# FFN up products of a two-layer encoder: two wider passes in place of three per weight block

## The chip, the cores and the metric

One core of one Trainium2 chip runs the whole program. The metric is the device time of one execution in microseconds (us). Before the change it is 1035.1 us, the median of three runs (1034.61 to 1035.34).

## The reference

A bidirectional encoder trunk of two layers over 256 tokens of width 1024, in float32. Each layer is an attention sublayer (three mixers) and a gated MLP. The change is in the MLP and in the way its input is laid out:

```python
def conv_gated_mlp(h, w_up, conv_w, w_down):
    u = h @ w_up                                   # 256 x 1024 by 1024 x 5632
    up = jnp.pad(u, ((0, 0), (pad, pad), (0, 0)))
    u = sum(up[:, t:t + S] * conv_w[t] for t in range(CONV_WIDTH))   # 3 taps over the tokens
    gate, val = jnp.split(u, 2, axis=-1)
    return (jax.nn.gelu(gate, approximate=True) * val) @ w_down

h = rms_norm(x, ffn_pre_norm[l])
x = x + rms_norm(conv_gated_mlp(h, w_up[l], ffn_conv[l], w_down[l]), ffn_post_norm[l])
```

## The kernel before

Every float32 product is made of three passes on TensorE. Both operands are split into a high part and a low part (`hi` is the value rounded to the matmul's type, `lo` is the rest), and `passes` (L1404 to L1408) sums low by high, high by low and high by high in one PSUM bank.

Weights come in pieces of up to 128 x 2048 values through a ring of three buffers. SyncE issues the DMA of piece n when the low part of piece n-3 has been made. ScalarE makes the high part of a piece (`split_hi`, L702), VectorE the low part (`split_lo`, L1051). Both engines walk through the same hand-written list of steps: in the step of piece n they split piece n+2, so TensorE can begin piece n+2 only when VectorE has come through that part of step n (TensorE waits for `lo_done`).

The MLP of a layer has 22 up pieces, c = 0 to 21, each with 8 blocks of 128 input channels for 256 output channels, and 11 down pieces. Even c is the gate half and odd c the value half of a unit u = c // 2. The order of the pieces is c0 to c5, down 0, c6, c7, down 1, and so on to c20, c21, down 8, down 9, down 10: the first six up pieces run without a down piece between them, then two up pieces and one down piece make a period.

- TensorE, up piece (`use_piece`, L1482 on): 16 pairs (k, j) of input block and half of the output channels; each pair is three passes with a 128 x 128 weight block as the stationary operand and 256 token columns of `hT_hi` or `hT_lo` as the moving one, 48 matmuls in all. A whole piece fills one PSUM bank, and four banks take turns (`up_half`), so piece c waits only for the scaling of piece c-4.
- TensorE, down piece: 24 matmuls of 512 columns. It waits for its weights and for `g_lo` of its unit (`gated_lo`, L1116).
- VectorE, step of an up piece: `scale_up` (L1104) reads the bank and multiplies by the token scales (the norm's root, one per token) into `up_scaled`; for odd c `gated` (L1111) of the unit before; `split_lo` of piece n+2; for even c `gated_lo` of unit u-2; then, after ScalarE's middle tap, two outer taps of the convolution for each of two halves (L1356, L1362). In the step of a down piece it only does `split_lo`.
- ScalarE, step of an up piece: `split_hi` of piece n+2, then, once `up_scaled` is there, two middle taps (L948); for odd c the gelu (L954) and `gated_hi` (L833) of the unit before.
- The last units: in the step of down 8, VectorE does `gated_lo` of unit 9 first, then `gated` and, after a split, `gated_lo` of unit 10.
- The turn into the MLP ("mid"): TensorE transposes x (`turn_ffn`, L1615 on) of two token halves t into PSUM in four pairs of blocks each; ScalarE makes `hT_hi` (L814), VectorE `hT_lo` (`ffn_lo`, L1078) in the order `FFN_LO`. Up piece 0 waits for the low parts of both t before it uses a pair.
- For c = 0 the token scales are only there when TensorE, in the middle of piece 1, has turned the roots (`turn_roots`); VectorE copies them in `scale_rows` (L1093) before it scales piece 0.

Of the kernel before, what the change touches and what calls it, by code (L numbers as in the profile page):

```python
# [8 lines left out]
F32 = mybir.dt.float32  # L9
F32R = mybir.dt.float32r  # L10
# [6 lines left out]
P = 128  # L17
# [249 lines left out]

FFN_FULL = [(t, pair) for t in range(NT) for pair in range(4)]
FFN_HI = FFN_FULL
FFN_LO = [(t, pair) for pair in range(4) for t in range(NT)]  # L270

NPAR = 3 * FT * 2 + 22 + 1
PRE_A, PRE_F, G_Q, G_KV, G_SUB, LAM = 132, 140, 148, 151, 153, 154
# [18 lines left out]
def build_trunk(nc, a, out):  # L292
    with ExitStack() as ctx:
# [6 lines left out]

        sb("pad_512", [P, 96])
        x = sb("x_rows", [P, NT, D])
        hT_hi = sb("hT_hi", [P, KD, SEQ], F32R)
        hT_lo = sb("hT_lo", [P, KD, SEQ], F32R)
        raw = sb("w_raw", [P, RING, 2048])
        w_hi = sb("w_hi", [P, RING, 2048], F32R)
        w_lo = sb("w_lo", [P, RING, 2048], F32R)
# [66 lines left out]
            sb("pad_six", [P, 5120], scope=six)  # L374
            par_rows = sb("par_rows", [44, 4 * DEPTH, P], scope=six)

        bank = [ctx.enter_context(nc.psum_tensor(f"bank{i}", [P, 512], F32)) for i in range(8)]
        S_BANK, O_BANK = (bank[4], bank[5]), bank[7]

        def t_bank(n):  # L380
# [34 lines left out]
        squares, rstd_done = sem("squares"), sem("rstd_done")  # L415
        ffn_squares = sem("ffn_squares")
        root_rows_ready, scales_full, up_scaled_done = sem("root_rows_ready"), sem("scales_full"), sem("up_scaled_done")
        lat_squares, lat_normed = sem("lat_squares"), sem("lat_normed")
        attn_means, latent_means, latent_roots = sem("attn_means"), sem("latent_means"), sem("latent_roots")
        head_means, head_roots = sem("head_means"), sem("head_roots")  # L420
# [76 lines left out]

        def turned_bank(t, k):

            return bank[((0, 1, 6, 7), (2, 3, 5, 0))[t][k // 2]][:, (k % 2) * P:(k % 2 + 1) * P]  # L500

        def up_half(c, j):

            if c == 0:
                return bank[(4, 2)[j]][:, 0:SEQ]
            return bank[4 + c % 4][:, j * SEQ:(j + 1) * SEQ]

        root_rows = xn[:, 0, 0:NT * P].rearrange("p (t q) -> p t q", t=NT)
        token_scale = xn[:, 0, 512:512 + SEQ]
# [165 lines left out]
        def _(act):  # L675
# [182 lines left out]
            for l in range(DEPTH):  # L858
                for step in STEPS:
# [64 lines left out]
                    elif what == "pv":  # L924
                        g = step[1]
                        if g < 4 or g >= 8:
                            act.wait_ge(o_full, l * NPV + (g + 1))
                            if g < 4:
                                nc.scalar.activation(mla_oT[:, g, 0, :], O_BANK[:, 0:SEQ], ACT.Copy).then_inc(o_hi, 1)
                            else:  # L930
                                nc.scalar.activation(dil_oT[:, g - 8, 0, :], O_BANK[:, 0:SEQ], ACT.Copy).then_inc(o_hi, 1)
                    elif what == "w":
                        n = step[1]
                        kind, c, k0, nk, cols = PIECES[n]
                        if n + 2 < NPIECE and n != UP0 - 1 and (l == 0 or n):
                            split_hi(l, n + 2)
                        if kind == "out" and c == 0 and k0 == 4:
                            for t in range(NT):
                                post_square(l, 0, t, 0)
                        if kind == "up":  # L940
                            u, b = c // 2, c % 2
                            act.wait_ge(up_scaled_done, l * 2 * NU + (c + 1))
                            if b == 1 and u >= 2:

                                act.wait_ge(g_lo_done, l * NU + (u - 1))
                            for j in range(2):
                                ch = 22 * b + 2 * u + j
                                last = nc.scalar.activation(conv[:, u % 2, b, j * SEQ:(j + 1) * SEQ], up_scaled[:, c % 2, j, :], ACT.Copy,  # L948
                                                            scale=par_all[:, l, 44 + ch:45 + ch])
                            last.then_inc(conv_mid, 1)  # L950
                            if b == 1:

                                act.wait_ge(conv_done, BASE + l * 2 * NU + c)
                                nc.scalar.activation(conv[:, u % 2, 0, :], conv[:, u % 2, 0, :], ACT.Gelu_apprx_tanh).then_inc(gelu_done, 1)  # L954
                                if u:
                                    gated_hi(l, u - 1)
                        elif kind == "down" and c == NU - 1 - LAG:
                            gated_hi(l, NU - 1)
                        elif kind != "down" and k0 + nk == K_TOTAL[kind] and kind not in BY_DVE:
                            f = first_of(n)  # L960
                            for m in range(f, f + tiles_of(n)):
                                empty_tile(l, m)
# [4 lines left out]
        def _(dve):  # L967
# [127 lines left out]

            def scale_up(l, n, c):

                dve.wait_ge(piece_used, l * NPIECE + (RING + n + 1))
                if c == 0:
                    scale_rows(l)  # L1100
                    for j in range(2):
                        last = V.tensor_tensor(up_scaled[:, c % 2, j, :], up_half(c, j), token_scale, ALU.mult)
                else:
                    last = V.tensor_tensor(up_scaled[:, c % 2, :, :], bank[4 + c % 4][:].rearrange("p (j q) -> p j q", j=2),  # L1104
                                           token_scale.rearrange("p (o q) -> p o q", o=1).broadcast_to([P, 2, SEQ]), ALU.mult)
                last.then_inc(up_scaled_done, 1)

            def gated(l, u):

# [145 lines left out]
            for l in range(DEPTH):  # L1255

                for step in STEPS:
# [68 lines left out]
                    elif what == "w":  # L1326
# [13 lines left out]
                        elif kind == "up":  # L1340
# [6 lines left out]
                                split_lo(l, n + 2)  # L1347
                            if b == 0 and u >= 2:
                                gated_lo(l, u - 2)
                            dve.wait_ge(conv_mid, l * 2 * NU + (c + 1))  # L1350
                            dve.drain()
                            cv, src = conv[:, u % 2, b, :], up_scaled[:, c % 2, :, :].rearrange("p j q -> p (j q)")
# [10 lines left out]
                                                              in1=cv[:, o:o + SEQ - 1], op0=ALU.mult, op1=ALU.add)  # L1363
                            last.then_inc(conv_done, 1)
                        elif last_pair:
                            gated_lo(l, NU - 2)
                            dve.drain()
                            gated(l, NU - 1)
                            split_lo(l, n + 2)
                            dve.drain()  # L1370
                            gated_lo(l, NU - 1)
# [3 lines left out]
        def _(pe):  # L1375
# [94 lines left out]
            def use_piece(l, n):  # L1470
# [10 lines left out]
                pe.wait_ge(lo_done, l * NPIECE + (n + 1 + RING))  # L1481
                if kind == "up":  # L1482
                    u, b = c // 2, c % 2
                    if c >= 4:

                        pe.wait_ge(up_scaled_done, l * 2 * NU + (c - 3))
                    order = [(k, j) for k in range(8) for j in range(2)] if c == 0 else [(k, j) for j in range(2) for k in range(8)]
                    for k, j in order:
                        if c == 0 and j == 0 and k % 2 == 0:
# [1 line left out]
                            pe.wait_ge(turn_emptied, l * NTURN + (TURN_BEFORE["ffn"] + last_of + 1))  # L1491
                        if c == 1 and (k, j) == (0, 1):
                            turn_roots(l)
                        last = passes(up_half(c, j), (hi[:, k, j * P:(j + 1) * P], lo[:, k, j * P:(j + 1) * P]),
                                      hT_hi[:, k, :], hT_lo[:, k, :], k == 0, k == 7)
                    last.then_inc(piece_used, 1)
                    return
                halves = 2 if cols == 1024 else 1
# [116 lines left out]
            def turn_ffn(l, t):  # L1615

                pe.wait_ge(tile_emptied_dve, BASE + l * N_DVE + emptied_by_dve(post_tile(0, 1, t)))
                for k in range(KD):
                    if k % 4 == 0:
                        pe.wait_ge(x_ready, l * 8 + (X_START + 2 * t + k // 4 + 1))  # L1620
                    if t == 1 and k == 6:
                        pe.wait_ge(turn_emptied, l * NTURN + (TURN_BEFORE["ffn"] + FFN_LO.index((0, 0)) + 1))
                    last = PE.transpose(turned_bank(t, k), x[:, t, k * P:(k + 1) * P], ident[:])
                    if k % 2 == 1:
                        last.then_inc(turn_full, 1)
# [183 lines left out]
```

## Time and profile before

| what | value |
|---|---|
| median of three runs | 1035.1 us |
| the profiled execution | 1034.86 us |
| its span, first to last instruction | 1033.1 us |
| granted TensorE clock, mean | 0.998 |
| TensorE / VectorE / ScalarE busy | 98% / 66% / 57% |
| first and last matmul of the up products | 329.8 and 1008.1 us |

All times in the rows below are microseconds from the start of the span. A matmul's shown duration includes the time through the array, so the rate of the engine is read from the distance between two starts, not from the duration. The same holds for neighbouring instructions of VectorE and ScalarE, which overlap by some hundredths of a microsecond. The two layers repeat one another 507.75 us apart.

### The profile page before, as it was taken

What the parts mean: (1) busy time and instruction counts of PE and PEld (TensorE: products, weight loads), DVE (VectorE), ACT (ScalarE), POOL (GpSimd) and SP (SyncE); (2) the same over time, 40 slices, a digit from 0 to 9 for tenths busy, and PEclk for the clock granted to TensorE, in tenths of its full rate; (3) what the DMA queues carried; (4) which work ended last, traced back from release to release, by engine and by line L of the source; (5) the groups of instructions that cost most, each with busy time, mean ns of one, the idle gap of its engine ahead of it and who ended that gap; (6) DMA issues with size and microseconds to landing.
All of it is one profiled execution on the core that took longest, in us unless ns stands there. A gap on an engine that the chain in (4) does not pass through costs nothing.

```text
span 1033.1 us, 15933 instructions
## 1 busy us (share of the span) xinstructions
PE 1014.2 (98%) x6244; PEld 908.9 (88%) x6244; DVE 679.4 (66%) x932; ACT 587.3 (57%) x859; POOL 131.8 (13%) x257
## 2 busy tenths in 40 slices
PE   8999999999999999999999999999999999999996
PEld 7889999888878999999888899998888789999995
DVE  5635566655586887878775355656555869787876
ACT  5657666555436655555475666565553457555543
POOL 3353114000002000000024221230000020000000
PEclk9999999999999999999999999999999999999999
DMA  8555445454445656555554544464345545555551
GB/s 250 185 174 155 123 144 165 158 164 163 143 140 166 204 167 200 178 190 186 166 181 151 173 123 128 149 204 164 128 154 174 176 143 167 200 176 192 186 181 41
DMA packets 106222, 170.79 MB, mean 165 GB/s; under 512 B 3377, under 2 KB 72804, under 8 KB 106148
## 3 DMA queue, kind: packets, MB, share of 16 engines
q1 hardware_dynamic: 104860, 166.88, 49.6%
q10 hardware_dynamic: 1208, 2.63, 0.7%
q8 instruction: 50, 0.82, 0.3%
q0 software_dynamic: 80, 0.26, 0.1%
q14 instruction: 24, 0.20, 0.1%
HBM read 168.72 MB, written 1.05 MB: 164 GB/s over the span
## 4 chain that ended last, share of the span: by engine, by line
PE 90%; DVE 5%; DVEq 2%; ACT 1%; issue 1%; DMA 1%; SPq 0%; POOL 0%; POOLq 0%; ACTq 0%
PE bank L1406 26%; PE bank L1408 26%; PE bank L1407 26%; PE bank L1757 2%; DVE w_lo L1051 1%; PE bank L1658 1%; PE bank L1679 1%; DVEq L1250 1%; PE bank L1750 1%; DVE merged L1251 1%; PE bank L1667 1%; PE bank L1695 1%; PE bank L1702 1%; PE bank L1747 1%; DMA w_raw<-in_w_in_dram 1%
## 5 line engine op out<-in xcount | busy, mean ns | idle before, releaser
L1051 DVE TENSOR_TENSOR w_lo<-w_raw,w_hi 128x2048 fp32r<-128x2048 f32 (+3 forms) x174 | 364.1, 2095 | 173.2 <-ACT w_hi L702 173.0
L702 ACT ACTIVATE w_hi<-w_raw 128x2048 fp32r<-128x2048 f32 (+3 forms) x174 | 304.6, 1752 | 60.9 <-PE bank L1408 59.2
L1406 PE MATMUL bank<-w_hi,hT_lo 128*128 128x512 f32 (+2 forms) x700 | 258.4, 369 | 2.1 <-DVE hT_lo L1125 1.3
L1408 PE MATMUL bank<-w_hi,hT_hi 128*128 128x512 f32 (+2 forms) x700 | 252.9, 361 | 0.0
L1407 PE MATMUL bank<-w_lo,hT_hi 128*128 128x512 f32 (+2 forms) x700 | 252.5, 361 | 0.0
L1406 PE MATMUL bank<-hT_hi,w_lo 128*128 128x256 f32 x704 | 199.4, 283 | 0.7 <-DVE hT_lo L1078 0.7
L1408 PE MATMUL bank<-hT_hi,w_hi 128*128 128x256 f32 x704 | 199.2, 283 | 0.0
L1407 PE MATMUL bank<-hT_lo,w_hi 128*128 128x256 f32 x704 | 199.2, 283 | 0.0
L1406 PEld LDWEIGHTS bank<-w_hi,hT_lo 128*128 128x128 f32 x700 | 131.5, 188 | 18.3 <-issue 3.5
L1408 PEld LDWEIGHTS bank<-w_hi,hT_hi 128*128 128x128 f32 x700 | 131.4, 188 | 14.1
L1407 PEld LDWEIGHTS bank<-w_lo,hT_hi 128*128 128x128 f32 x700 | 131.6, 188 | 13.0
L1406 PEld LDWEIGHTS bank<-hT_hi,w_lo 128*128 128x128 f32 x704 | 135.1, 192 | 1.7 <-issue 1.1
L1407 PEld LDWEIGHTS bank<-hT_lo,w_hi 128*128 128x128 f32 x704 | 135.1, 192 | 0.6
L1408 PEld LDWEIGHTS bank<-hT_hi,w_hi 128*128 128x128 f32 x704 | 135.1, 192 | 0.0
L948 ACT ACTIVATE conv_out<-up_scaled,par_all 128x256 f32<-128x256 f32 x88 | 40.1, 502 | 147.3 <-DVE up_scaled L1104 136.5
L612 POOL TENSOR_SCALAR mean_squares<-small 128x1 f32<-128x1 f32 x12 | 7.8, 654 | 603.2 <-ACT x_normed L847 587.7
L1406 PE MATMUL bank<-w_hi,g_lo 128*128 128x512 f32 x176 | 68.9, 391 | 2.2 <-DVE g_lo L1116 2.2
L1407 PE MATMUL bank<-w_lo,g_hi 128*128 128x512 f32 x176 | 68.7, 390 | 0.0
L1408 PE MATMUL bank<-w_hi,g_hi 128*128 128x512 f32 x176 | 68.5, 389 | 0.0
L1104 DVE TENSOR_TENSOR up_scaled<-bank,x_normed 128x512 f32<-128x512 f32 x42 | 29.0, 691 | 59.1 <-PE bank L1408 59.1
L601 POOL TENSOR_TENSOR rope_a<-stage,cosT 128x96 f32<-128x96 f32 (+1 forms) x40 | 28.7, 717 | 164.9 <-ACT stage L721 136.2
L1356 DVE SCALAR_TENSOR_TENSOR conv_out<-up_scaled,par_all,conv_out 128x255 f32<-128x255 f32 x88 | 38.7, 481 | 6.0 <-ACT conv_out L948 2.1
(215 smaller groups left out, 1249.9 us busy)
## 6 DMA issues: line engine op xcount, KB each, us to landing
w_raw<-in_w_up_dram SPq DMA_DIRECT2D x44, 1024.0 KB, 4.9
w_raw<-in_w_in_dram SPq DMA_DIRECT2D x36, 1024.0 KB, 5.0
w_raw<-in_w_in_dram SPq DMA_DIRECT2D x36, 768.0 KB, 4.3
w_raw<-in_w_down_dram SPq DMA_DIRECT2D x22, 1024.0 KB, 4.8
w_raw<-in_w_out_dram SPq DMA_DIRECT2D x8, 1024.0 KB, 4.9
w_raw<-in_w_in_dram SPq DMA_DIRECT2D x8, 672.0 KB, 4.0
w_raw<-in_w_branch_mla_dram SPq DMA_DIRECT2D x4, 1024.0 KB, 4.8
w_raw<-in_w_branch_diff_dram SPq DMA_DIRECT2D x4, 1024.0 KB, 5.1
```

The source lines that it names most:

```text
L601: nc.gpsimd.tensor_tensor(ca, xr, c, ALU.mult)
L702: nc.scalar.activation(w_hi[:, n % RING, 0:nk * cols], raw[:, n % RING, 0:nk * cols], ACT.Copy).then_inc(hi_done, 1)
L948: last = nc.scalar.activation(conv[:, u % 2, b, j * SEQ:(j + 1) * SEQ], up_scaled[:, c % 2, j, :], ACT.Copy, scale=par_all[:, l, 44 + ch:4 ...
L1051: V.tensor_tensor(w_lo[:, n % RING, s], raw[:, n % RING, s], w_hi[:, n % RING, s].bitcast(F32), ALU.subtract).then_inc(lo_done, 1)
L1104: last = V.tensor_tensor(up_scaled[:, c % 2, :, :], bank[4 + c % 4][:].rearrange("p (j q) -> p j q", j=2), token_scale.rearrange("p (o q) ...
L1250: dve.drain()
L1251: last = V.tensor_tensor(merged[:, t, s], merged[:, t, s], gs, ALU.add)
L1356: V.scalar_tensor_tensor(out=cv[:, o + 1:o + SEQ], in0=src[:, o:o + SEQ - 1], scalar=par_all[:, l, ch:ch + 1], in1=cv[:, o + 1:o + SEQ], o ...
L1406: PE.matmul(dst, lhs[1], rhs_hi, start=start, stop=False)
L1407: PE.matmul(dst, lhs[0], rhs_lo, start=False, stop=False)
L1408: return PE.matmul(dst, lhs[0], rhs_hi, start=False, stop=stop)
L1757: last = PE.transpose(T_BANK[:, b * P:(b + 1) * P], probs[:, i % 2, b * P:(b + 1) * P], ident[:])
```

## The change

The high and the low part of the MLP's input now lie side by side in one buffer, `hT`, and one 512-column pass multiplies a block's high weights with both; the low weights go over the high input alone, in a 256-column pass into the first half of the same bank. Each up piece now fills two banks of 512 columns, and two such pairs of banks take turns, so piece c waits for the summing of piece c-2. ScalarE copies the second half of both banks to `up_scaled`, VectorE adds the first half to it, and a further VectorE instruction multiplies by the token scales. The order of the low parts of `hT` and the banks of the transposes change at the turn into the MLP, because banks 4 and 5 are now those of piece 0. `gated_lo` of unit 9 moves from the step of down 8 to the step of c21, ahead of its taps.

```diff
-FFN_LO = [(t, pair) for pair in range(4) for t in range(NT)]
+FFN_LO = [(0, 0), (0, 1), (1, 0), (1, 1), (0, 2), (1, 2), (0, 3), (1, 3)]
...
-        hT_hi = sb("hT_hi", [P, KD, SEQ], F32R)
-        hT_lo = sb("hT_lo", [P, KD, SEQ], F32R)
+        hT = sb("hT", [P, KD, 2, SEQ], F32R)
+        hT_hi, hT_lo = hT[:, :, 0, :], hT[:, :, 1, :]
...
-            return bank[((0, 1, 6, 7), (2, 3, 5, 0))[t][k // 2]][:, (k % 2) * P:(k % 2 + 1) * P]
+            return bank[((0, 1, 6, 7), (2, 3, 0, 1))[t][k // 2]][:, (k % 2) * P:(k % 2 + 1) * P]
+        def up_banks(c):
+            return up_bank[:, 2 * (c % 2):2 * (c % 2) + 2, :]
...
(ScalarE, step of an up piece, behind split_hi)
+                            act.wait_ge(piece_used, l * NPIECE + (RING + n + 1))
+                            if c >= 2:
+                                act.wait_ge(conv_done, BASE + l * 2 * NU + (c - 1))
+                            nc.scalar.activation(up_scaled[:, c % 2, :, :], up_banks(c)[:, :, SEQ:2 * SEQ], ACT.Copy).then_inc(up_copied, 1)
                             act.wait_ge(up_scaled_done, l * 2 * NU + (c + 1))
...
(VectorE, scale_up)
-                dve.wait_ge(piece_used, l * NPIECE + (RING + n + 1))
+                dve.wait_ge(up_copied, l * 2 * NU + (c + 1))
+                sums = up_scaled[:, c % 2, :, :]
+                V.tensor_tensor(sums, sums, up_banks(c)[:, :, 0:SEQ], ALU.add).then_inc(up_summed, 1)
                 if c == 0:
                     scale_rows(l)
-                    for j in range(2):
-                        last = V.tensor_tensor(up_scaled[:, c % 2, j, :], up_half(c, j), token_scale, ALU.mult)
-                else:
-                    last = V.tensor_tensor(up_scaled[:, c % 2, :, :], bank[4 + c % 4][:]..., token_scale..., ALU.mult)
-                last.then_inc(up_scaled_done, 1)
+                dve.drain()
+                V.tensor_tensor(sums, sums, token_scale..., ALU.mult).then_inc(up_scaled_done, 1)
...
(VectorE, step of an up piece, ahead of the taps; and the step of down 8)
+                            if c == 2 * NU - 1:
+                                gated_lo(l, NU - 2)
...
-                            gated_lo(l, NU - 2)
...
(TensorE, up piece)
-                    if c >= 4:
-                        pe.wait_ge(up_scaled_done, l * 2 * NU + (c - 3))
+                    if c >= 2:
+                        pe.wait_ge(up_summed, l * 2 * NU + (c - 1))
...
-                        last = passes(up_half(c, j), (hi[:, k, j * P:(j + 1) * P], lo[:, k, j * P:(j + 1) * P]),
-                                      hT_hi[:, k, :], hT_lo[:, k, :], k == 0, k == 7)
+                        into = up_banks(c)[:, j, :]
+                        PE.matmul(into, hi[:, k, j * P:(j + 1) * P], hT[:, k, :, :].rearrange("p s q -> p (s q)"),
+                                  start=k == 0, stop=False, skip_group_check=True)
+                        last = PE.matmul(into[:, 0:SEQ], lo[:, k, j * P:(j + 1) * P], hT_hi[:, k, :], start=False, stop=k == 7,
+                                         skip_group_check=True)
...
(TensorE, turn_ffn)
-                    if t == 1 and k == 6:
-                        pe.wait_ge(turn_emptied, l * NTURN + (TURN_BEFORE["ffn"] + FFN_LO.index((0, 0)) + 1))
+                    if t == 1 and k in (4, 6):
+                        pe.wait_ge(turn_emptied, l * NTURN + (TURN_BEFORE["ffn"] + FFN_LO.index((0, k // 2 - 2)) + 1))
```

## Rows read from the trace of the kernel before

**Rows 1.** The page, busy time of each engine, share of the span, instructions.

```profile
PE 1014.2 (98%) x6244; PEld 908.9 (88%) x6244; DVE 679.4 (66%) x932; ACT 587.3 (57%) x859; POOL 131.8 (13%) x257
```

**Rows 2.** Timeline of TensorE around one up and one down piece: start, duration, instruction.

```profile
376.12 0.28 PE L1406 MATMUL bank<-hT_hi,w_lo 128*128 128x256 f32 x1
...
381.88 0.40 PE L1406 MATMUL bank<-w_hi,g_lo 128*128 128x512 f32 x1
...
387.34 0.28 PE L1406 MATMUL bank<-hT_hi,w_lo 128*128 128x256 f32 x1
```

**Rows 3.** Timeline of VectorE over one period of three pieces; idle time and releaser in brackets.

```profile
376.32 0.69 DVE L1104 TENSOR_TENSOR up_scaled<-bank,x_normed 128x512 f32<-128x512 f32 x1 [3.60 <-PE bank L1408]
376.93 2.28 DVE L1051 TENSOR_TENSOR w_lo<-w_raw,w_hi 128x2048 fp32r<-128x2048 f32 x1
379.12 1.09 DVE L1116 TENSOR_TENSOR g_lo<-conv_out,g_hi 128x512 fp32r<-128x512 f32 x1
380.31 0.88 DVE L1356 SCALAR_TENSOR_TENSOR conv_out<-up_scaled,par_all,conv_out 128x255 f32<-128x255 f32 x2
381.26 0.88 DVE L1362 SCALAR_TENSOR_TENSOR conv_out<-up_scaled,par_all,conv_out 128x255 f32<-128x255 f32 x2
382.08 0.69 DVE L1104 TENSOR_TENSOR up_scaled<-bank,x_normed 128x512 f32<-128x512 f32 x1
382.69 0.68 DVE L1111 TENSOR_TENSOR conv_out<-conv_out 128x512 f32<-128x512 f32 x1
383.29 2.28 DVE L1051 TENSOR_TENSOR w_lo<-w_raw,w_hi 128x2048 fp32r<-128x2048 f32 x1
...
387.42 2.28 DVE L1051 TENSOR_TENSOR w_lo<-w_raw,w_hi 128x2048 fp32r<-128x2048 f32 x1
393.30 0.69 DVE L1104 TENSOR_TENSOR up_scaled<-bank,x_normed 128x512 f32<-128x512 f32 x1 [3.60 <-PE bank L1408]
```

**Rows 4.** Timeline at the end of the first layer, TensorE and VectorE.

```profile
506.27 1.06 DVE L1116 TENSOR_TENSOR g_lo<-conv_out,g_hi 128x512 fp32r<-128x512 f32 x1
...
507.47 0.47 PE L1406 MATMUL bank<-w_hi,g_lo 128*128 128x512 f32 x1 [1.11 <-DVE g_lo L1116]
...
507.78 0.39 PE L1407 MATMUL bank<-w_lo,g_hi 128*128 128x512 f32 x1
...
510.41 1.07 DVE L1116 TENSOR_TENSOR g_lo<-conv_out,g_hi 128x512 fp32r<-128x512 f32 x1
```

**Rows 5.** Timeline of eight transposes of 128 columns.

```profile
523.11 1.04 PE L1551 MATMUL bank<-ident,x_rows 128*128 128x128 f32 x8
```

**Rows 6.** ScalarE's groups by form: busy time, mean ns of one, idle time before.

```profile
L776 ACT ACTIVATE probsT<-bank 128x512 f32<-128x512 f32 x40 | 23.9, 597 | 31.5 <-PE bank L1757 31.5
```

**Rows 7.** Timeline at the turn into the MLP, first layer.

```profile
328.40 4.39 DVE L1078 SCALAR_TENSOR_TENSOR hT_lo<-bank,par_all,hT_hi 128x128 fp32r<-128x128 f32 x16
...
329.83 0.35 PE L1406 MATMUL bank<-hT_hi,w_lo 128*128 128x256 f32 x1 [0.34 <-DVE hT_lo L1078]
```

**Rows 8.** Timeline of VectorE in the first six up pieces, first layer.

```profile
336.56 2.28 DVE L1051 TENSOR_TENSOR w_lo<-w_raw,w_hi 128x2048 fp32r<-128x2048 f32 x1
339.25 0.49 DVE L1093 COPY x_normed<-bank 128x128 f32<-128x128 f32 x2 [0.42 <-PE bank L1467]
...
359.34 0.69 DVE L1104 TENSOR_TENSOR up_scaled<-bank,x_normed 128x512 f32<-128x512 f32 x1 [0.34 <-PE bank L1408]
```

**Rows 9.** Timeline of ScalarE in the same stretch and in the period.

```profile
341.42 1.90 ACT L702 ACTIVATE w_hi<-w_raw 128x2048 fp32r<-128x2048 f32 x1
...
345.01 1.28 ACT L954 ACT_TABLE_LOAD   x1
...
383.62 0.62 ACT L954 ACTIVATE conv_out<-conv_out 128x512 f32<-128x512 f32 x1
384.14 1.13 ACT L833 ACTIVATE g_hi<-conv_out 128x512 fp32r<-128x512 f32 x1
```

**Rows 10.** The page, DMA issues: count, size, median us from issue to landing.

```profile
w_raw<-in_w_up_dram SPq DMA_DIRECT2D x44, 1024.0 KB, 4.9
```

More of the change, by code:

```diff
@@ L375, in build_trunk @@
             par_rows = sb("par_rows", [44, 4 * DEPTH, P], scope=six)
-        bank = [ctx.enter_context(nc.psum_tensor(f"bank{i}", [P, 512], F32)) for i in range(8)]
+        bank = [ctx.enter_context(nc.psum_tensor(f"bank{i}", [P, 512], F32)) for i in range(4)]
+        up_bank = ctx.enter_context(nc.psum_tensor("up_bank", [P, 4, 512], F32))
+        bank += [up_bank[:, i, :] for i in range(4)]
         S_BANK, O_BANK = (bank[4], bank[5]), bank[7]
@@ L417, in build_trunk @@
         root_rows_ready, scales_full, up_scaled_done = sem("root_rows_ready"), sem("scales_full"), sem("up_scaled_done")
+        up_copied, up_summed = sem("up_copied"), sem("up_summed")
         lat_squares, lat_normed = sem("lat_squares"), sem("lat_normed")
@@ L498, in turned_bank @@
         def turned_bank(t, k):
-            return bank[((0, 1, 6, 7), (2, 3, 5, 0))[t][k // 2]][:, (k % 2) * P:(k % 2 + 1) * P]
[L502 to L506, printed above, removed]
+            return bank[((0, 1, 6, 7), (2, 3, 0, 1))[t][k // 2]][:, (k % 2) * P:(k % 2 + 1) * P]
+        def up_banks(c):
+            return up_bank[:, 2 * (c % 2):2 * (c % 2) + 2, :]
         root_rows = xn[:, 0, 0:NT * P].rearrange("p (t q) -> p t q", t=NT)
@@ L1096, in scale_up @@
             def scale_up(l, n, c):
-                dve.wait_ge(piece_used, l * NPIECE + (RING + n + 1))
+                dve.wait_ge(up_copied, l * 2 * NU + (c + 1))
+                sums = up_scaled[:, c % 2, :, :]
+                V.tensor_tensor(sums, sums, up_banks(c)[:, :, 0:SEQ], ALU.add).then_inc(up_summed, 1)
                 if c == 0:
                     scale_rows(l)
-                    for j in range(2):
-                        last = V.tensor_tensor(up_scaled[:, c % 2, j, :], up_half(c, j), token_scale, ALU.mult)
-                else:
-                    last = V.tensor_tensor(up_scaled[:, c % 2, :, :], bank[4 + c % 4][:].rearrange("p (j q) -> p j q", j=2),
-                                           token_scale.rearrange("p (o q) -> p o q", o=1).broadcast_to([P, 2, SEQ]), ALU.mult)
-                last.then_inc(up_scaled_done, 1)
+                dve.drain()
+                V.tensor_tensor(sums, sums, token_scale.rearrange("p (o q) -> p o q", o=1).broadcast_to([P, 2, SEQ]), ALU.mult).then_inc(up_scaled_done, 1)
             def gated(l, u):
```

## The prediction

> **What bounds the kernel now.** I began with the busy times of the page: TensorE is busy 98% of the span, VectorE 66%, ScalarE 57% [rows 1]. So TensorE sets the time, and an edit that shortens its work helps only as long as nobody else becomes late. The busy share can't say whether that holds in the MLP, so I went to the timelines of that stage.
>
> TensorE first. An up piece runs from 376.12 to 381.88, 5.76 us for 48 matmuls of 256 columns: 0.120 each. The down piece runs to 387.34, 5.46 us for 24 matmuls of 512 columns: 0.2275 each [rows 2]. The next up piece follows without a gap. A period of two up pieces and one down piece is 2 x 5.76 + 5.46 = 16.98 us, and VectorE's rows repeat at exactly that distance, 376.32 and 393.30 [rows 3].
>
> VectorE next, because TensorE can't begin a piece before VectorE has made its low part. Let E be the moment at which VectorE starts on an even up piece (376.32). It is 0.20 behind the start of TensorE's next matmul (376.12), so "TensorE's next piece starts at X" and "its consumer starts at X + 0.20" are the same event. From E on VectorE runs: scaling at +0, `split_lo` of the down piece +0.61, `g_lo` +2.80, taps +3.99 and +4.94, scaling of the odd piece +5.76, `gated` +6.37, `split_lo` of the next even piece +6.97 to +9.25, taps, `split_lo` +11.10 to +13.38, and then 3.60 idle [rows 3]. The first 5.76 of these have no idle time in them. The low part that TensorE needs at 387.34 (+11.02) is there at +9.25. What TensorE adds between a release and its steady rate is read at the end of the layer: `g_lo` is ready at 507.33, the first matmul starts at 507.47, the second at 507.78, so 0.14 and then 0.31 in place of 0.23, together 0.22 [rows 4]. The real slack of VectorE's chain is thus 11.02 - 9.25 - 0.22 = 1.55 us in a period of 16.98. The 3.60 idle are not spare in the same sense: they lie behind the instruction that TensorE waits for.
>
> **The change part by part.**
>
> *Passes.* A pair (k, j) was 3 x 0.120 = 0.360. Now it is one pass of 512 and one of 256 columns, 0.2275 + 0.120 = 0.3475 [rows 2]. The columns are the same, 768; what goes is what a matmul costs beside its columns, 0.0125. Sixteen pairs make a piece 5.56 instead of 5.76; all 44 pieces give at most 704 x 0.0125 = 8.8 us. Bounds for a pair, since no row alternates the two widths: 0.335 (0.2275 and bare columns, 0.2275 - 0.120 = 0.1075) and 0.360 (no gain). I take the sum of the two measured distances.
>
> How much a weight load costs decides this price. Eight transposes of 128 columns take 1.04, of which 0.28 is the last one's duration: (1.04 - 0.28) / 7 = 0.109 between starts [rows 5]. If such a load stood ahead of each stream, a matmul of 256 columns would take 0.109 + 0.1075 = 0.216; the rows show 0.120, so the load lies under the matmul before it, and taking one away gives back little. The Trainium skill (TensorE: Matmul & The Clock Gate, Part 3, The mechanism) says that a weight load overlaps matmuls in flight only when its row group differs; here all loads use the whole array, so by that rule each removed load would be worth its full price. The trace disagrees with it.
>
> *ScalarE's copy.* A link that was not in the chain. ScalarE waits for the piece, then copies 512 values from PSUM; the same form takes 0.597 [rows 6], and the hand-over adds about 0.03: +0.63 before VectorE can start. For odd pieces VectorE comes late anyway and the copy is hidden.
>
> *The add and the drain.* VectorE had one instruction of 512 for the scaling, 0.69, and 0.61 to the next start. Now it has an add (0.69, then the drain; drains in the period cost 0.07 to 0.10, as 380.31 + 0.88 to 381.26, so 0.78 to the next start) and a multiplication with all operands in SBUF, like `gated` (0.68, 0.60 to the next start) [rows 3]. That is 1.38 where 0.61 stood: +0.77 for each up piece. Bounds: 0.60 (a bare distance again, no drain) and 0.90.
>
> *The period.* All of this falls on VectorE's chain from E: copy 0.63, add, multiplication to +2.01, `split_lo` (2.19 to the next start), `g_lo` +4.20 to +5.29, taps +5.39 and +6.34, the odd piece's add +7.16, multiplication +7.94, `gated` +8.54, `split_lo` +9.14 to +11.42. TensorE would have wanted it at 5.56 + 5.46 - 0.20 = +10.82; it goes on at 11.42 + 0.22 = +11.64. The slack of 1.55 has been turned into a stall of 0.82, of which 0.15 comes already ahead of the down piece (its `g_lo` is ready at +5.29, TensorE effectively goes on at +5.51 instead of +5.36). The loop closes: the next even piece ends 5.56 later, and the next E is at 11.64 + 5.56 + 0.20 = +17.40. So a period takes 17.40 where it took 16.98: the copy, the add and the drain ask for 2.17, the shorter even piece gives 0.20 back and the slack 1.55; **+0.42**. The odd piece's 0.20 is lost in the stall. The rest of VectorE's step ends at +15.57 and is not late. ScalarE isn't late either: its `split_hi` for the even piece ends near +4.9, its copy of the odd piece can run at +5.56, and behind that come taps, gelu and `g_hi` as before [rows 9].
>
> *The first six up pieces.* There the relief of a down piece is missing and VectorE was nearly full before: it idled 0.34 ahead of piece 4 [rows 8]. Here each step must be followed. Piece 0 starts at 330.20, not 329.83: four low parts follow one another 0.271 apart ((4.39 - 0.32) / 15), and the pair that piece 0 needs is now finished by the sixth instruction, 328.40 + 5 x 0.271 + 0.31 = 330.07, plus 0.13 [rows 7]. Piece 2 ends at 330.28 + 3 x 5.56 + 0.43 for the roots = 347.39. VectorE comes out of `split_lo` at 338.84, adds piece 0, takes the roots at about 339.5 (339.25 before) [rows 8], and ends its taps at 343.6. ScalarE is held by the taps of piece 0, does `split_hi` until 343.5 [rows 9], and only then copies piece 1. From there: add at 344.15, `split_lo` of piece 3 to 347.81, piece 3 goes on at 348.03 (stall 0.64) and ends at 353.59. ScalarE loads the gelu's table (1.28) [rows 9], splits to 350.3 and copies piece 2 to 350.9; `split_lo` of piece 4 ends at 354.59 (stall 1.22). Piece 5 is released at 360.71 (stall 0.56), down 0 by its `g_lo` at 367.50 (stall 1.23; ScalarE's copy of piece 4 had to wait for its `split_hi`, to 362.8), piece 6 at 373.63 (stall 0.67). E of piece 6 comes at 379.61; it was 376.32 [rows 3]. Check: stalls 4.32, later start 0.37, seven shorter pieces -1.40: **+3.29**.
>
> *The periods* from E of piece 6 to E of piece 20: 7 x 0.42 = **+2.94**.
>
> *The end of a layer.* Before, TensorE waited 1.11 for `g_lo` of unit 9 ahead of down 9, and the last down piece ended 23.29 behind E of piece 20. Now `g_lo` of unit 9 follows `split_lo` ahead of the taps: ready at +12.42, down 9 effectively from +12.64 (before +12.37), end +18.10. But the taps, `gated`, a split and `g_lo` of unit 10 come behind it, one after the other as before [rows 4]: taps from +12.52 to +14.29, `gated` +14.36, split +14.97, `g_lo` ready at +18.42, down 10 effectively from +18.64, end +24.10: **+0.81**. Behind the taps, `g_lo` of unit 9 would be ready at +14.3 and the end 1.4 later; the move is worth that, but doesn't bring back what VectorE's lateness costs.
>
> *At no cost.* Two banks in turn instead of four: TensorE needs the sum of piece c-2, and that is there 2 us and more ahead in each step above. The order of transposes: pairs 2 and 3 of the second half wait for low parts at 328.95 and 329.5, their high parts come 0.1 later, and piece 0 asks for them only at 333; uncovered it would be that 0.1. Weight transfers: 4.9 us to landing [rows 10], issued when the low part of piece n-3 is made, over a period ahead of their use; if this failed, ScalarE's split would wait and each late microsecond would go to TensorE. The wider layout of `hT` is read and written by the same instructions; I find no row that prices the stride and take 0, with 0.1 us either way.
>
> *Sum.* 3.29 + 2.94 + 0.81 = 7.04 a layer, 14.1 for two. The profiled execution took 1034.86; it stands 0.24 below the median. 1034.86 + 14.1 = **1049.0 us**.
>
> **The rivals.** *A: TensorE sets the pace and the gain arrives.* For it: 98% busy, and VectorE idles 3.60 in each period. Against it: that idle time is behind the instruction on which TensorE waits. It decides at the chain: if copy, add and multiplication asked for 0.82 less than 2.17 + 0.20 in a period, no stall would be left; for mere equality with before, 0.42 less. Then 8.8 us are gained and 2 x 0.37 lost at the start of piece 0: 1034.86 - 8.1 = 1026.8.
>
> *B: the mixed pair costs three passes.* The two passes take 0.360 or more, because a load under 256 columns followed by a wide pass hides less. Each up piece is 5.76 again; the chain through the even piece lengthens by 0.20 in each period and by about as much in each early step, some 1.6 a layer: 1052.2.
>
> *C: loads at their full price*, the mechanism that the rows speak against: a pair costs 0.360 - 0.109 = 0.251, a piece 4.02. VectorE's chain stays, only the even piece in the loop shrinks by 1.54 more, about 8 times in a layer: 1049.0 - 2 x 8 x 1.54 = 1024.4. This is where the rule of the Trainium skill (the page on TensorE, as above) would lead.
>
> *D: the VectorE steps cost about as much less as to end near the old time*, with the chain still in the lead: 0.77 down to 0.50. Two by 0.27 off a period of 17.40 is 16.86, 0.12 under the old one, and some 2 of the 4.1 lost early and at the end remain: about 1037.
>
> **How the numbers follow.** Forecast 0.73, A 0.09, B 0.12, C 0.02, D 0.04. The range: from the forecast down, the extra VectorE time at 0.65 instead of 0.77 takes 0.24 off each of 7 periods and 0.12 off about 6 early and last steps, 4.8 us for both layers, and the pair at 0.335 takes 0.2 off each piece in the chain, 3.3 more: 1040.9. Upward, B and the extra time at 0.85: 1052.2 + 3.2 = 1055.4. I give 1040.0 to 1056.0. It leaves out A, C and part of D, and the far sides, together about 0.2. About 0.2% is what a measurement of this kernel tells from no change; faster by more: A, C, a part of D, 0.12; within: 0.02; slower: 0.86.
>
> **What would show it.** The distance between starts of a pair: 0.3475. VectorE without a long wait for the copy in odd steps, and E to E at 17.40. TensorE waiting for `w_lo` (L1051's successor) 0.6 to 0.7 ahead of each even piece and for `g_lo` near 0.1 ahead of down pieces, where before it waited for neither. E of piece 6 near 379.6. Wrong would be the forecast if E to E came at 16.58 (rival A), if the pair measured 0.36 (B) or 0.25 (C), or if TensorE waited for `up_summed`, which I hold to be free.

## The result: 1048.9 us, slower by 1.3%, and the profile after

The changed kernel takes 1048.9 us (median of four runs, 1048.76 to 1049.06), the kernel before 1035.2 in the same session. The ratio is 1.0134, 95% interval 1.0120 to 1.0147. The forecast was 1049.0.

From the page of the changed kernel, busy times and then the chain that ended last:

```profile
PE 1017.2 (97%) x5540; PEld 869.4 (83%) x5540; DVE 708.7 (68%) x974; ACT 610.8 (58%) x903; POOL 130.8 (12%) x257
...
PE 67%; DVE 20%; DVEq 6%; ACT 4%; issue 2%; DMA 1%; SPq 0%; POOL 0%; POOLq 0%; ACTq 0%
```

and the chain of the kernel before, for comparison:

```profile
PE 90%; DVE 5%; DVEq 2%; ACT 1%; issue 1%; DMA 1%; SPq 0%; POOL 0%; POOLq 0%; ACTq 0%
```

TensorE has 704 instructions less and is still busy 97% of the span [rows 1]; the busy share says nearly nothing. The chain says it: TensorE's part fell from 90% to 67%, VectorE's rose from 5% to 20%.

What TensorE waited for (us in total, times, longest), changed kernel:

```profile
PE up_bank L1500 <- DVE w_lo L1057: 7.4, 20, 0.8
PE bank L1411 <- DVE g_lo L1120: 3.6, 4, 1.4
...
PE up_bank L1500 <- DVE hT L1084: 0.3, 2, 0.2
```

Twenty waits for low weights that were not there before, ten in each layer, and none for `up_summed`: two banks in turn were enough. This view undercounts a wait, since a matmul's shown duration runs 0.16 into it, and the first matmul behind it is slow (0.34 to the next start, 390.89 to 391.23 below, where others take 0.23).

One period of the changed kernel, ScalarE's copy, VectorE and TensorE:

```profile
379.41 0.60 ACT L947 ACTIVATE up_scaled<-up_bank 128x512 f32<-128x512 f32 x1 [2.72 <-PE up_bank L1502]
...
380.04 0.69 DVE L1106 TENSOR_TENSOR up_scaled<-up_scaled,up_bank 128x512 f32<-128x512 f32 x1 [2.52 <-ACT up_scaled L947]
380.82 0.69 DVE L1110 TENSOR_TENSOR up_scaled<-up_scaled,x_normed 128x512 f32<-128x512 f32 x1
381.43 2.29 DVE L1057 TENSOR_TENSOR w_lo<-w_raw,w_hi 128x2048 fp32r<-128x2048 f32 x1
383.64 1.09 DVE L1120 TENSOR_TENSOR g_lo<-conv_out,g_hi 128x512 fp32r<-128x512 f32 x1
384.82 0.88 DVE L1362 SCALAR_TENSOR_TENSOR conv_out<-up_scaled,par_all,conv_out 128x255 f32<-128x255 f32 x2
385.77 0.88 DVE L1368 SCALAR_TENSOR_TENSOR conv_out<-up_scaled,par_all,conv_out 128x255 f32<-128x255 f32 x2
386.57 0.68 DVE L1106 TENSOR_TENSOR up_scaled<-up_scaled,up_bank 128x512 f32<-128x512 f32 x1
387.34 0.69 DVE L1110 TENSOR_TENSOR up_scaled<-up_scaled,x_normed 128x512 f32<-128x512 f32 x1
387.95 0.68 DVE L1115 TENSOR_TENSOR conv_out<-conv_out 128x512 f32<-128x512 f32 x1
388.55 2.28 DVE L1057 TENSOR_TENSOR w_lo<-w_raw,w_hi 128x2048 fp32r<-128x2048 f32 x1
...
390.89 0.50 PE L1500 MATMUL up_bank<-hT,w_hi 128*128 128x512 f32 x1 [0.31 <-DVE w_lo L1057]
391.23 0.28 PE L1502 MATMUL up_bank<-hT,w_lo 128*128 128x256 f32 x1
391.34 0.40 PE L1500 MATMUL up_bank<-hT,w_hi 128*128 128x512 f32 x1
...
396.64 0.40 PE L1500 MATMUL up_bank<-hT,w_hi 128*128 128x512 f32 x1
...
396.84 0.60 ACT L947 ACTIVATE up_scaled<-up_bank 128x512 f32<-128x512 f32 x1 [2.71 <-PE up_bank L1502]
```

Read it against [rows 3]. E, the moment at which an even up piece's consumer starts, is now the start of ScalarE's copy. From E, 379.41, the low weights of the next even piece are done at 390.83, +11.42, where they were done at +9.25. TensorE begins the piece 0.06 later, and E comes again at 396.84: a period of 17.43 in place of 16.98. VectorE still idles 2.52 in it, behind the instruction that TensorE waits for and ahead of the copy.

### The profile page after: what moved, and what is told of

It is laid out like the page before. It is cut to its first block, busy times and chain, and to the rows that moved or that the text cites. A ratio compares the mean times of both kernels' runs of the same rounds, so it can differ in the third digit from the quotient of the medians.

```text
span 1047.3 us, 14699 instructions
## 1 busy us (share of the span) xinstructions
PE 1017.2 (97%) x5540; PEld 869.4 (83%) x5540; DVE 708.7 (68%) x974; ACT 610.8 (58%) x903; POOL 130.8 (12%) x257
## 4 chain that ended last, share of the span: by engine, by line
PE 67%; DVE 20%; DVEq 6%; ACT 4%; issue 2%; DMA 1%; SPq 0%; POOL 0%; POOLq 0%; ACTq 0%
PE bank L1411 15%; PE bank L1413 15%; PE bank L1412 15%; DVE w_lo L1057 9%; PE up_bank L1500 7%; PE up_bank L1502 3%; DVE up_scaled L1110 3%; DVE up_scaled L1106 3%; PE up_bank L1765 2%; DVEq L1357 2%; ACT w_hi L703 1%; PE up_bank L1666 1%; PE up_bank L1687 1%; DVEq L1254 1%; ACT up_scaled L947 1%
## 5 line engine op out<-in xcount | busy, mean ns | idle before, releaser
L1411 PE MATMUL bank<-w_hi,hT 128*128 128x512 f32 (+2 forms) x700 | 258.4, 369 | 2.1 <-DVE hT L1129 1.3
L1500 PE MATMUL up_bank<-hT,w_hi 128*128 128x512 f32 x704 | 252.2, 402 | 7.8 <-DVE w_lo L1057 7.4
L1413 PE MATMUL bank<-w_hi,hT 128*128 128x512 f32 (+2 forms) x700 | 252.9, 361 | 0.0
L1412 PE MATMUL bank<-w_lo,hT 128*128 128x512 f32 (+2 forms) x700 | 252.5, 361 | 0.0
L1502 PE MATMUL up_bank<-hT,w_lo 128*128 128x256 f32 x704 | 197.6, 281 | 0.0
L1500 PEld LDWEIGHTS up_bank<-hT,w_hi 128*128 128x128 f32 x704 | 132.2, 188 | 48.3 <-DVE w_lo L1057 16.0
L1411 PEld LDWEIGHTS bank<-w_hi,hT 128*128 128x128 f32 x700 | 131.5, 188 | 18.2 <-issue 3.5
L1413 PEld LDWEIGHTS bank<-w_hi,hT 128*128 128x128 f32 x700 | 131.4, 188 | 14.0
L1412 PEld LDWEIGHTS bank<-w_lo,hT 128*128 128x128 f32 x700 | 131.7, 188 | 13.0
L1502 PEld LDWEIGHTS up_bank<-hT,w_lo 128*128 128x128 f32 x704 | 133.0, 189 | 0.0
L1106 DVE TENSOR_TENSOR up_scaled<-up_scaled,up_bank 128x512 f32<-128x512 f32 x44 | 30.1, 684 | 43.4 <-ACT up_scaled L947 43.2
L1411 PEld LDWEIGHTS bank<-w_hi,g_lo 128*128 128x128 f32 x176 | 33.0, 188 | 15.6 <-issue 7.4
```

The source lines that it names most:

```text
L1106: V.tensor_tensor(sums, sums, up_banks(c)[:, :, 0:SEQ], ALU.add).then_inc(up_summed, 1)
L1411: PE.matmul(dst, lhs[1], rhs_hi, start=start, stop=False)
L1412: PE.matmul(dst, lhs[0], rhs_lo, start=False, stop=False)
L1413: return PE.matmul(dst, lhs[0], rhs_hi, start=False, stop=stop)
L1500: PE.matmul(into, hi[:, k, j * P:(j + 1) * P], hT[:, k, :, :].rearrange("p s q -> p (s q)"), start=k == 0, stop=False, skip_group_check=True)
L1502: last = PE.matmul(into[:, 0:SEQ], lo[:, k, j * P:(j + 1) * P], hT_hi[:, k, :], start=False, stop=k == 7, skip_group_check=True)
```

## The experiments

Two theories stood against each other. *Chain*: the copy, the add and the drain make VectorE deliver low weights too late, and the order of its work counts. *Others*: the passes themselves, the two banks in turn, ScalarE's copy wherever it stands, or the mere amount of VectorE's work.

**Without the scaling** (it leaves out the multiply by the token scales for pieces 1 to 21):

```diff
-                V.tensor_tensor(sums, sums, up_banks(c)[:, :, 0:SEQ], ALU.add).then_inc(up_summed, 1)
+                added = V.tensor_tensor(sums, sums, up_banks(c)[:, :, 0:SEQ], ALU.add)
+                added.then_inc(up_summed, 1)
+                if c >= 1:
+                    dve.drain().then_inc(up_scaled_done, 1)
+                    return
```

> The changed kernel without VectorE's drain-and-multiply by the token scales for pieces 1 to 21 (the sum is passed on unscaled; only piece 0 is scaled, so the output is not the reference's). It takes about 0.6 us out of each VectorE step. Theory (VectorE's chain from the copy over add, multiply, taps to the low weights sets the period): the period falls from 17.44 us to TensorE's own 2 x 5.65 + 5.46 = 16.8 or close to it, the waits for low weights ahead of even pieces vanish, and the time falls by some 18 us, to about 1030. Rival (the loss comes from ScalarE's copy and the two pairs of banks taking turns, or from the passes): the multiply is covered, and the time stays at 1047 to 1049.

Measured: 1031.5 us, ratio to the kernel before 0.9968 (0.9956 to 0.9980). ScalarE's copies of even pieces, one period apart:

```profile
393.17 0.60 ACT L947 ACTIVATE up_scaled<-up_bank 128x512 f32<-128x512 f32 x1 [3.34 <-PE up_bank L1506]
...
409.97 0.60 ACT L947 ACTIVATE up_scaled<-up_bank 128x512 f32<-128x512 f32 x1 [3.38 <-PE up_bank L1506]
```

16.80, TensorE's own pace (two up pieces of 5.65 and a down piece of 5.46 are 16.76). The copy, the add, the banks and the passes are all still there. So none of them is the loss by itself: leaving out one short VectorE instruction per piece takes the whole loss in the periods away.

**Three passes again**, everything else as changed:

```diff
-                        PE.matmul(into, hi[:, k, j * P:(j + 1) * P], hT[:, k, :, :].rearrange("p s q -> p (s q)"),
+                        PE.matmul(into[:, 0:SEQ], hi[:, k, j * P:(j + 1) * P], hT_hi[:, k, :],
                                   start=k == 0, stop=False, skip_group_check=True)
+                        PE.matmul(into[:, SEQ:2 * SEQ], hi[:, k, j * P:(j + 1) * P], hT_lo[:, k, :],
+                                  start=False, stop=False, skip_group_check=True)
```

> The changed kernel, but the 512-column pass is issued as two passes of 256 columns into the two halves of the bank, so each pair has three passes again; everything else as changed. It prices the wide pass alone. In the changed kernel a mixed pair takes 0.353 between starts, three passes take 0.360. Theory: a piece grows by 0.1 us, of which one in each period and nearly all early ones count: +2 us, about 1051. Rival (mixed widths cost TensorE time, so that the wide pass is part of the loss): the time falls below 1048. Rival (a weight load is worth its full price, 0.109): the time rises by 10 us or more.

Measured: 1051.0 us, 2.1 above the changed kernel. The wide pass is a small gain, and no part of the loss. Loads at their full price, which would have cost 10 us or more here, are excluded.

**The low part of unit 9 behind the taps again:**

```diff
-                            if c == 2 * NU - 1:
-                                gated_lo(l, NU - 2)
...
                         elif last_pair:
+                            gated_lo(l, NU - 2)
                             dve.drain()
```

> The changed kernel with the low part of unit 9 back where it was, in the step of down 8, behind the taps of piece 21. Theory: down 9 is released later by taps and outer work, about 1.4 us a layer: +2.7 us, 1051.6. Rival (the move buys nothing, because down 10 waits for its own low part in any case): 1049.

Measured: 1054.1 us, 5.2 more than the changed kernel where 2.7 were expected, and an unusually wide spread: the four runs took 1050.9, 1053.4, 1054.8 and 1055.4 us, at mean granted clocks of 0.999, 0.997, 0.994 and 0.993. TensorE at the start of down 9 in the first layer:

```profile
516.40 0.76 PE L1410 MATMUL bank<-w_hi,g_lo 128*128 128x512 f32 x1 [3.30 <-DVE g_lo L1120]
516.97 0.63 PE L1411 MATMUL bank<-w_lo,g_hi 128*128 128x512 f32 x1
517.39 0.63 PE L1412 MATMUL bank<-w_hi,g_hi 128*128 128x512 f32 x1
517.82 0.63 PE L1410 MATMUL bank<-w_hi,g_lo 128*128 128x512 f32 x1
```

and the stretches before and behind it (start and end, length, busy time of each engine, then the granted clock, DMA share and GB/s):

```profile
508.00:512.00 4.00, 4.00 (x19) 3.31 (x18) 3.83 (x7) 1.59 (x5) 0.00 (x0) 1.00 0.42 151
516.00:520.00 4.00, 3.60 (x9) 2.91 (x10) 3.82 (x4) 2.38 (x2) 0.00 (x0) 0.57 0.18 66
520.00:524.00 4.00, 4.00 (x20) 3.27 (x19) 1.89 (x2) 0.21 (x1) 0.00 (x0) 1.00 0.74 223
```

Here 3.30 us of waiting were followed by a granted clock of 0.57, so mostly the lower level, 1.2 GHz, and 512 columns took 0.43 from start to start instead of 0.2275. In the second layer of the same run the wait was as long, and the clock stayed at 1.00:

```profile
PE bank L1410 <- DVE g_lo L1120: 3.3, 1, 3.3
...
1034.00:1037.00 3.00, 3.00 (x15) 2.47 (x14) 2.91 (x3) 1.14 (x1) 0.00 (x0) 1.00 0.00 0
```

The two layers tell the two parts of the price apart. From E of piece 20 to ScalarE's first read of the last down piece it is 21.55 us in the second layer, 1.25 more than in the changed kernel (20.30), and 23.15 in the first, 2.86 more (20.29). So the move that the change makes is worth 1.25 us a layer by the order of work, 2.5 in all, close to the 2.7 expected and to the 2.0 of the fastest run. The rest, 2.7 of the 5.2 us, came with the lower clock. The changed kernel, whose wait there is 1.4 us, showed 0.998 or 0.999 in all four of its runs.

**The copy twice**, on even pieces from 6 on, and on odd pieces from 7 on:

```diff
+                            if c >= 6 and c % 2 == 0:          # in the other kernel == 1
+                                nc.scalar.activation(xn[:, 1, (c // 2 % 2) * 512:(c // 2 % 2) * 512 + 512]..., up_banks(c)[:, :, SEQ:2 * SEQ], ACT.Copy)
                             nc.scalar.activation(up_scaled[:, c % 2, :, :], up_banks(c)[:, :, SEQ:2 * SEQ], ACT.Copy).then_inc(up_copied, 1)
```

> The changed kernel with ScalarE's copy of even pieces from 6 on made twice (the first time to a scratch buffer), some 0.50 us more ahead of the add. Theory (the copy of an even piece lies in the chain): each of 8 even pieces a layer adds 0.50, +8 us, 1057. Rival (the copy is hidden behind VectorE's or TensorE's other work): within 1 us of 1049.

> The same doubling of the copy for odd pieces from 7 on. Theory (VectorE comes to the odd piece late, so that copy is covered): within 0.5 us of 1048.9. Rival (every copy is in the chain): +8 us.

Measured: 1056.5 us for even pieces, 7.6 above the changed kernel, and 1049.0 for odd ones, no difference. The same instruction costs nearly its full distance of 0.50 in one place and nothing in the other. In the even run the next period's copy comes 17.91 later, where it was 17.43:

```profile
379.20 0.60 ACT L948 ACTIVATE x_normed<-up_bank 128x512 f32<-128x512 f32 x1 [2.71 <-PE up_bank L1504]
379.70 0.59 ACT L949 ACTIVATE up_scaled<-up_bank 128x512 f32<-128x512 f32 x1
...
397.11 0.60 ACT L948 ACTIVATE x_normed<-up_bank 128x512 f32<-128x512 f32 x1 [2.70 <-PE up_bank L1504]
```

**Low weights first.** VectorE's work is only reordered; the same edit was made to the kernel before as a control:

```diff
+                            early = c >= 4 and b == 0
+                            if splits and early:
+                                split_lo(l, n + 2)
                             scale_up(l, n, c)
...
-                            if splits and c:
+                            if splits and c and not early:
                                 split_lo(l, n + 2)
```

> The changed kernel with one reordering on VectorE: for even pieces from 4 on, the low weights of the piece after next are made ahead of the add and not behind the multiply, in the time in which VectorE waits for the piece. No work is added or left out. Theory (the period is lost to the order of work in VectorE's chain, not to its amount): 2.2 us leave the chain between the end of the even piece and the low weights of the next one, the period falls to TensorE's own 16.8, and the time falls by about 11 us, to 1038. Rival (VectorE's amount of work or its memory traffic is too large now): 1045 or more.

> The kernel before with the same reordering of VectorE, as a control. Theory (there the chain had 1.55 us of slack): no change, 1035.2 within 0.5. Rival (the reordering is a gain by itself): 1033 or less.

Measured: the changed kernel so reordered 1038.2 us, 10.7 less; the kernel before so reordered 1034.8 beside 1034.9, no change. VectorE from one even piece to the next:

```profile
391.44 4.49 DVE L1057 TENSOR_TENSOR w_lo<-w_raw,w_hi 128x2048 fp32r<-128x2048 f32 x2
396.47 0.69 DVE L1106 TENSOR_TENSOR up_scaled<-up_scaled,up_bank 128x512 f32<-128x512 f32 x1 [0.54 <-ACT up_scaled L947]
397.25 0.69 DVE L1110 TENSOR_TENSOR up_scaled<-up_scaled,x_normed 128x512 f32<-128x512 f32 x1
397.86 1.07 DVE L1120 TENSOR_TENSOR g_lo<-conv_out,g_hi 128x512 fp32r<-128x512 f32 x1
```

Both low weights now lie back to back (x2) in the time that was idle, 2.52 before, 0.54 now, and E follows E at 16.79. That the same amount of work runs at TensorE's pace when it stands elsewhere shows that order, not amount, was the loss in the periods. What is left against the kernel before is 3.4 us. By the traces the first six pieces are 3.0 longer in each layer than before, the seven periods together 1.3 shorter, and the end of the layer 0.07 longer.

**And the copies of pieces 1 and 2 ahead of the high weights:**

```diff
+                        late = kind == "up" and c in (1, 2)
-                        if n + 2 < NPIECE and n != UP0 - 1 and (l == 0 or n):
+                        if n + 2 < NPIECE and n != UP0 - 1 and (l == 0 or n) and not late:
                             split_hi(l, n + 2)
...
+                            if late:
+                                split_hi(l, n + 2)
```

> As the reordered changed kernel (low weights ahead of the add for even pieces from 4 on), and for pieces 1 and 2 ScalarE copies the piece ahead of making high weights. Theory (in the first six pieces the copy waits behind 1.9 us of high weights): another 3.5 us, about 1034.6, level with the kernel before. Rival (the early pieces are bound by VectorE's amount of work): no gain over the reordering alone.

Measured: 1035.1 us beside 1034.9, ratio 1.0002 (0.9993 to 1.0012): level with the kernel before. The waits for low weights ahead of pieces 4 and 5 are gone. In the MLP of the first layer these remain:

```profile
364.98 0.47 PE L1417 MATMUL bank<-w_hi,g_lo 128*128 128x512 f32 x1 [0.58 <-issue]
...
371.47 0.50 PE L1506 MATMUL up_bank<-hT,w_hi 128*128 128x512 f32 x1 [0.78 <-DVE w_lo L1060]
...
506.64 0.47 PE L1417 MATMUL bank<-w_hi,g_lo 128*128 128x512 f32 x1 [0.59 <-DVE g_lo L1123]
...
512.72 0.47 PE L1417 MATMUL bank<-w_hi,g_lo 128*128 128x512 f32 x1 [0.38 <-DVE g_lo L1123]
```

The first six pieces now take 1.3 to 1.5 more than before in a layer, and the periods give 1.3 back: that is why the kernel is level and not faster.

**Two more moves, together and one alone,** and the first of these kernels with three passes:

```diff
-                            early = c >= 4 and b == 0
+                            early = c == 5 or (c >= 4 and b == 0)      # not in the one with the gating move alone
...
-                            if b == 1 and u >= 1:
-                                gated(l, u - 1)
...
                             last.then_inc(conv_done, 1)
+                            if b == 0 and u >= 1:
+                                gated(l, u - 1)
```

> The reordered changed kernel with the copy of pieces 1 and 2 first, and two more moves on VectorE: the low weights of the piece after next are made first for piece 5 too, and the gating product of the unit before moves from the odd step to the end of the even step, where VectorE idles 1.2 us. No work is added or left out. Theory (what is left are single waits: 0.78 ahead of piece 6, about 0.5 and 0.6 ahead of down 9 and down 10, in each layer): 1.3 to 1.5 us a layer, so 1035.1 - 2.8 = 1032.3, faster than the kernel before by 0.25%. Rival (VectorE's work of the first six pieces is the bound, and the order only shifts the waits): 1034.5 or more.

> The same, with the 512-column pass again as two passes of 256 columns. Here TensorE sets the pace in most pieces, so the wide pass shows what it is worth. Theory: 0.360 - 0.3535 = 0.0065 for each of 704 pairs, 4.6 us, less what falls into the waits that are left: 4 us above the two-pass version. By the forecast's price of 0.0125 a pair it would be 8.8 us. Rival (mixed widths give nothing): equal.

> The kernel with low weights and early copies first (1035.1), plus the gating product moved to the end of the even step, without the move for piece 5. Theory (the run with both moves lost 1.8 us because low weights ahead of piece 5's add delay its taps and with them ScalarE's high weights for piece 7): the 1.7 us wait ahead of piece 7 is gone, and the time is 1034.3 to 1035.2. Rival (the early gating product itself costs): 1036.5 or more.

Measured: both moves 1036.9 us, ratio 1.0016 (1.0007 to 1.0025); the gating move alone 1034.65 beside 1034.88, ratio 0.9999 (0.9990 to 1.0008). The expectation of 1032.3 for both moves was wrong by 4.6, and its rival, that the order only shifts the waits (1034.5 or more), is what came. The wait ahead of piece 6 went, and a longer one came ahead of piece 7. Rows of the run with both moves, of the three engines:

```profile
371.80 0.91 ACT L957 ACTIVATE conv_out<-up_scaled,par_all 128x256 f32<-128x256 f32 x2 [4.26 <-DVE up_scaled L1113]
...
376.10 4.49 DVE L1060 TENSOR_TENSOR w_lo<-w_raw,w_hi 128x2048 fp32r<-128x2048 f32 x2 [1.45 <-ACT w_hi L703]
...
378.45 0.50 PE L1506 MATMUL up_bank<-hT,w_hi 128*128 128x512 f32 x1 [1.70 <-DVE w_lo L1060]
```

With low weights first, piece 5 is scaled 2.2 later than with the gating move alone; ScalarE, which works in order, stands 4.26 waiting for that (2.05 with the gating move alone) ahead of the high weights of piece 7; VectorE then waits 1.45 for these. The chain runs through both engines, so what is won ahead of one link on VectorE is paid for behind ScalarE. Without the move for piece 5 the loss was gone, as expected. With three passes the kernel with both moves takes 1040.3, 3.4 more, close to the 4 that were expected and far from the 8.8 of the forecast's price.

## Why the prediction was right, step by step

*What bounds it.* Right. The idle 3.60 of VectorE was not spare; the slack was 1.55, and the runs with low weights first and with the copy twice show the chain directly: the same work in another order takes the loss of the periods away, and 0.50 more in the even step costs 7.6 us in 16 pieces, in the odd step nothing.

*The period.* Forecast 17.40, measured 17.43. On VectorE every distance came as priced: copy and hand-over 0.63, add 0.78, multiply 0.61, low weights ready at +11.42 as forecast. Two terms beyond it were off and cancelled. A pair of passes takes 0.353, not 0.3475: from 391.34 to 396.64 are 15 pairs, 5.30 / 15. That is the mis-sized term of the sum: the wide pass gains about half of what the forecast gave it (0.0067 for each pair instead of 0.0125), and a piece is 5.65, not 5.56. The sum of the two distances of [rows 2] was too low. And TensorE started 0.06 behind its low weights, not 0.14. The forecast had read the 0.14 from a wait for `g_lo` [rows 4] and used it for `w_lo`; behind `g_lo` it is 0.14 in the changed kernel too, after a wait of only 0.36 (below). The 0.15 forecast ahead of the down piece did not show as a wait: `g_lo` was ready at 384.73, and TensorE came to it at 384.87.

```profile
518.81 1.06 DVE L1120 TENSOR_TENSOR g_lo<-conv_out,g_hi 128x512 fp32r<-128x512 f32 x1
...
520.01 0.47 PE L1411 MATMUL bank<-w_hi,g_lo 128*128 128x512 f32 x1 [0.36 <-DVE g_lo L1120]
```

*The first six pieces.* Forecast +3.29. E of piece 6 comes at 379.41; the run stands 0.15 ahead of the one before at the turn into the MLP (327.81 against 327.96 for the second half's transposes), so +3.24. Inside it the distribution was off: the wait of 0.64 ahead of piece 3 didn't come, since the pieces ahead of it were longer and VectorE could add piece 1 0.36 earlier than forecast. The waits came to 3.7 instead of 4.3, and the seven shorter pieces gave 0.8 instead of 1.4. These two go together: where VectorE's chain sets the end, a longer piece only eats into the wait behind it. The second layer, though, has only +2.90. The difference is a pause of 0.43 in VectorE's row of work in the taps of piece 4, for which the profile gives no reason; in the second layer the same instruction comes 0.34 earlier after the one before it, and so does everything behind it:

```profile
368.34 0.88 DVE L1368 SCALAR_TENSOR_TENSOR conv_out<-up_scaled,par_all,conv_out 128x255 f32<-128x255 f32 x2 [0.43 <-issue]
```

*The end of a layer.* Forecast +0.81. The first tile of the last down piece was read by ScalarE at 521.68, 20.29 behind E of piece 20 (501.39), before at 19.38 (495.18 to 514.56): +0.91.

```profile
521.68 0.60 ACT L848 ACTIVATE x_normed<-bank 128x512 f32<-128x512 f32 x1 [0.60 <-PE bank L1413]
```

Before:

```profile
514.56 0.60 ACT L847 ACTIVATE x_normed<-bank 128x512 f32<-128x512 f32 x1
```

*The sum, and the luck in it.* The same three stretches in both layers, us more than before:

| stretch | forecast | first layer | second layer |
|---|---|---|---|
| up to E of piece 6 | 3.29 | 3.24 | 2.90 |
| seven periods | 2.94 | 3.12 | 3.10 |
| end of the layer | 0.81 | 0.91 | 0.92 |
| sum | 7.04 | 7.27 | 6.92 |

The two profiled executions are 14.2 apart, 14.1 were forecast. Each term was right to within 0.4 us. That the total came out within 0.1 is luck: the periods and the end were forecast 0.3 too low in each layer, and the first six pieces of the second layer 0.4 too high.

*The move of unit 9* was priced at 1.4 a layer. Where the clock held it is worth 1.25. The forecast had left out that the clock can fall behind a wait of 3.3 us, which cost 1.6 more in the one layer where the trace shows it (2.86 in all).

*At no cost.* Banks in turn, transfers and the wider layout: no wait for `up_summed` and none for a transfer appeared in the MLP. For the layout by itself no run was made.

*The rivals.* A, TensorE at its own pace, came when I took the multiply out: 1031.5 instead of the 1026.8 that it was given; 704 x (0.353 - 0.3475) = 3.9 us of the difference are the pair's price. B was in the right direction with half its size, C (a pair at 0.251) is excluded by the 0.353, D didn't happen: no VectorE instruction was cheaper.

Not settled: whether some order of the work brings the changed kernel clearly below the kernel before. Copying pieces 1 and 2 first won the last 3.4 us back; that order and the two others built on it ended level or above (1035.1, 1034.65 and 1036.9).

## What to carry to other kernels

Measure the slack of a helper engine at the instruction that the busy engine waits for, and not by its idle time: 2.2 us of new work fitted into 3.6 us of idle time in amount and not in order. Where a change adds a link to such a chain, first look for work that can move from behind the link into the wait ahead of it; here that gave back 10.7 of 13.7 us without a single instruction less. And before splitting off work to save passes on TensorE, price the passes: 704 matmuls fewer were worth 2.1 us in the changed kernel and 3.4 where TensorE set the pace in most pieces, because a load cost almost nothing beside the matmul before it.

## What the runs showed of the hardware

- A stream that alternates 512 and 256 columns runs at 0.353 a pair, 0.006 more than the sum of the distances in uniform streams (0.2275 and 0.120).
- One wait of 3.30 us was followed by about 3 us with 512 columns at 0.43 from start to start, near half speed (granted clock 0.57 over 4 us); another of 3.3 us in the same run was not (1.00).
- Behind a wait the first 512-column matmul takes longer until the next one: 0.34 in an up piece, 0.31 in a down piece, instead of 0.23.
- From the end of VectorE's `w_lo` to TensorE's first matmul it was 0.05 to 0.06 (waits of 0.3 to 0.8 us), from the end of `g_lo` 0.14 to 0.15 (waits of 0.36 to 1.4 us). So it went by what was waited for and not by the length of the wait; why, no run shows.
